# The feed-forward input GEMMs of a hybrid decoder layer, with the activations as the stationary operand

## The reference, cut to what matters

```
def swiglu(h, w_in, w_out):
    a, b = jnp.split(h @ w_in, 2, axis=-1)      # h: 256 x 2048, w_in: 2048 x 11008
    return (jax.nn.silu(a) * b) @ w_out         # w_out: 5504 x 2048

h = modulate(x, norm_ffn1[l], sh1, sc1)
x = x + 0.5 * g1 * swiglu(h, w_ffn1_in[l], w_ffn1_out[l])
...                                             # the mixer
h = modulate(x, norm_ffn2[l], sh3, sc3)
x = x + 0.5 * g3 * swiglu(h, w_ffn2_in[l], w_ffn2_out[l])
```

## Time and profile before

| what | value |
|---|---|
| median of three runs | 2865.64 us (2865.18 to 2868.14) |
| the profiled execution, first to last instruction | 2863.1 us |
| TensorE busy | 2574.2 us, 90% |
| VectorE busy | 1781.1 us, 62% |
| ScalarE busy | 997.2 us, 35% |
| transfers | 567.49 MB, mean 198 GB/s |
| mean granted TensorE clock | 0.938 of full |

### The profile page before, as it was taken

One profiled execution on the slowest core, in us unless ns is written; L12 is line 12 of the kernel. 1 busy time (PEld: TensorE's weight loads), 2 busy tenths in 40 slices (PEclk: granted clock), 3 DMA queues, 4 the chain that ended last, 5 costly groups with the idle time before them and its releaser, 6 DMA issues. The chain is left out here.

```text
span 2863.1 us, 47785 instructions
## 1 busy us (share of the span) xinstructions
PE 2574.2 (90%) x20140; PEld 2536.1 (89%) x20140; DVE 1781.1 (62%) x1754; ACT 997.2 (35%) x690; POOL 221.1 (8%) x214
## 2 busy tenths in 40 slices
PE   5589989999989788788999988989799999999897
PEld 5589989999989688688899988989699989999897
DVE  5666656767656656888777775656575545444444
ACT  1044433333333322323334443333344333333333
POOL 0010000460000112232400000000000000000000
PEclk6589999999999879889999999999899999999999
DMA  8777767777767552233346655756487645555451
GB/s 297 265 221 264 264 205 240 261 251 263 247 203 246 187 176 89 89 118 103 118 150 213 226 191 190 236 191 246 136 276 252 228 148 194 180 182 185 144 183 70
DMA packets 386137, 567.49 MB, mean 198 GB/s; under 512 B 12709, under 2 KB 209829, under 8 KB 385253
## 3 DMA queue, kind: packets, MB, share of 16 engines
q1 hardware_dynamic: 385332, 560.33, 58.1%
q0 software_dynamic: 688, 5.51, 0.6%
HBM read 561.59 MB, written 4.19 MB: 198 GB/s over the span
## 5 line engine op out<-in xcount | busy, mean ns | idle before, releaser
L264 PE MATMUL gps<-hs,whi 128*128 128x256 f32 x9088 | 1687.8, 288 | 161.9 <-DVE wlo L774 103.8
L264 PEld LDWEIGHTS gps<-hs,whi 128*128 128x128 f32 x9088 | 1446.9, 196 | 174.6 <-DVE wlo L774 107.2
L774 DVE TENSOR_TENSOR wlo<-raw,whi 128x2048 fp32r<-128x2048 f32 x400 | 925.3, 2314 | 858.9 <-ACT whi L520 858.8
L264 PE MATMUL gps<-hs,wlo 128*128 128x256 f32 x4544 | 1301.5, 286 | 0.0
L520 ACT ACTIVATE whi<-raw 128x2048 fp32r<-128x2048 f32 x400 | 765.3, 1914 | 1318.2 <-PE gps L264 1314.9
L264 PEld LDWEIGHTS gps<-hs,wlo 128*128 128x128 f32 x4544 | 888.6, 196 | 0.0
L264 PE MATMUL gps<-ffs,whi 128*128 128x256 f32 x2752 | 506.6, 287 | 27.8 <-DVE ffs L840 23.9
L264 PEld LDWEIGHTS gps<-ffs,whi 128*128 128x128 f32 x2752 | 434.6, 194 | 33.3 <-issue 24.4
L791 DVE SCALAR_TENSOR_TENSOR acc<-raw,cact,acc 128x512 f32<-128x512 f32 x508 | 384.7, 757 | 15.6
L264 PE MATMUL gps<-ffs,wlo 128*128 128x256 f32 x1376 | 392.2, 285 | 0.0
L264 PEld LDWEIGHTS gps<-ffs,wlo 128*128 128x128 f32 x1376 | 267.3, 194 | 0.0
(11 more groups left out here) (216 smaller groups left out, 1328.8 us busy)
## 6 DMA issues: line engine op xcount, KB each, us to landing
raw<-in_w_ffn_in_dram SPq DMA_DIRECT2D x336, 512.0 KB
raw<-in_w_ada_dram SPq DMA_DIRECT2D x144, 1024.0 KB
raw<-in_w_in_dram SPq DMA_DIRECT2D x80, 1024.0 KB
raw<-in_w_ffn_out_dram SPq DMA_DIRECT2D x56, 1024.0 KB
raw<-in_w_ffn_out_dram SPq DMA_DIRECT2D x40, 768.0 KB
raw<-in_w_a_proj_dram SPq DMA_DIRECT2D x16, 1024.0 KB
raw<-in_w_b_glu_dram SPq DMA_DIRECT2D x32, 512.0 KB
raw<-in_w_out_dram SPq DMA_DIRECT2D x16, 1024.0 KB
```

What stands on the lines that cost most here:

```text
L264: return pe.matmul(out, lhsT, rhs, start=start, stop=stop, skip_group_check=True)
L774: dve.tensor_tensor(wlo[:, mpos % SPLIT, :, :], raw[:, pos % RING, :, :], whi[:, mpos % SPLIT, :, :].bitcast(F32), ALU.subtract).then_inc( ...
```

## The change

In the pair phases the roles on TensorE are exchanged: `slab_pair` holds a 128 x 128 block of activations (128 features by 128 tokens, two token halves c) and moves 512 weight columns, so a slab is 2 x 4 x 3 = 24 matmuls of 512 columns. The result has tokens on the partitions. A body is now 512 gate columns in g = 0 and the matching 512 of the other half in g = 1; each slab is one transfer of 1 MB. ACT evacuates g = 0 alone (Silu to `half`, 1024 elements a partition), DVE multiplies g = 1 with it (`gated`, 1024), and the four blocks of 128 columns are turned back by eight 128 x 128 transposes on TensorE into `mps` (`turn`), then copied and split into `ffs` by ACT and DVE, 1024 elements each. A body's `turn` is issued on TensorE inside the next body (or the next output phase): after the first token half of its slab 0, or after the first column block of an output phase. It waits for `gated`. The output phase no longer waits for all of `ffs` at its start: each of its slabs waits for the bodies that made its rows. The narrow body moves 384 columns in all eight slabs. First bodies after a norm or an output phase, and first bodies of output phases, are taken out of the loops.

```diff
@@ class/plan: start is counted in tiles of ffs; Run has pt @@
@@ sync @@
+                            if ph.evac == "pair":
+                                width = COLS - P if ph.narrow else COLS
+                                parts = [(dst[:, :, 0:width],
+                                          w[:, k0:k0 + kc, bass.ds(ph.col + i * COLS + g * ph.pair, width)])]
...
@@ scalar, evacuate @@
-                    act.wait_ge(sem("prod_free"), r.p + i * 2 + g + 1)
-                    act.activation(sil[:, :, :], out[:, 0:2, :], ACT.Silu).then_inc(sem("silu_ready"), 1)
-                    act.wait_ge(psum_free(b), q)
...
+                    if g == 0:
+                        act.wait_ge(sem("prod_free"), r.p + i + 1)
+                        act.activation(half[:, :, 0:width], out.rearrange("p (c h) s -> p c (h s)", c=2)[:, :, 0:width],
+                                       ACT.Silu).then_inc(psum_free(b), 1)
+                    else:
+                        act.wait_ge(sem("ff_turned"), r.pt + i + 1)
+                        turned = mps[:, 0:2, :].rearrange("p a (b s) -> p (a b) s", b=2)
+                        act.activation(ffs[:, bass.ds(ph.start + 4 * i, blocks), 0, :], turned[:, 0:blocks, :], ACT.Copy
+                                       ).then_inc(sem("ff_hi"), 1)
@@ vector, evacuate @@
+                    if g == 1:
+                        dve.wait_ge(slab_done, m_end)
+                        dve.wait_ge(psum_free(0), q)
+                        dve.tensor_tensor(gated[:, :, 0:width], half[:, :, 0:width],
+                                          out.rearrange("p (c h) s -> p c (h s)", c=2)[:, :, 0:width], ALU.mult
+                                          ).then_inc(psum_free(b), 1)
+                        dve.wait_ge(sem("ff_hi"), r.p + i + 1)
+                        turned = mps[:, 0:2, :].rearrange("p a (b s) -> p (a b) s", b=2)
+                        at_ = bass.ds(ph.start + 4 * i, blocks)
+                        dve.tensor_tensor(ffs[:, at_, 1, :], turned[:, 0:blocks, :],
+                                          ffs[:, at_, 0, :].bitcast(F32), ALU.subtract).then_inc(sem("prod_free"), 1)
@@ tensor @@
-                if ph.moving == "ff":
-                    pe.wait_ge(sem("prod_free"), r.p + 1)
+                def slab_pair(g, s, mp, k0):
+                    width = COLS - P if ph.narrow else COLS
+                    for c in range(2):
+                        tok = slice(P * c, P * c + P)
+                        out = gps[:, g, 2 * c:2 * c + 2, :].rearrange("p h s -> p (h s)")[:, 0:width]
+                        for k in range(ph.chunks[s]):
+                            hi, lo = whi[:, mp % SPLIT, k, 0:width], wlo[:, mp % SPLIT, k, 0:width]
+                            xh, xl = moving[:, k0 + k, 0, tok], moving[:, k0 + k, 1, tok]
+                            mm(pe, out, xh, hi, k0 + k == 0, False)
+                            mm(pe, out, xh, lo, False, False)
+                            ins = mm(pe, out, xl, hi, False, k0 + k == NT - 1)
+                        yield ins
...
+                def turn(p, q, blocks):
+                    pe.wait_ge(psum_free(1), q)
+                    pe.wait_ge(sem("prod_free"), p + 1)
+                    for b in range(blocks):
+                        for c in range(2):
+                            at_ = S * (b % 2) + P * c
+                            ins = pe.transpose(mps[:, b // 2, at_:at_ + P], gated[:, c, P * b:P * b + P], ident[:, :])
+                    ins.then_inc(sem("ff_turned"), 1)
...
+                            if ph.moving == "ff" and head and g == 0:
+                                pe.wait_ge(sem("prod_free"), ff_from[0] + (k0 + ph.chunks[s] + 3) // 4 + 1)
+                            parts = slab_pair(g, s, mp, k0) if ph.evac == "pair" else slab_plain(g, s, mp, k0)
+                            for j, ins in enumerate(parts):
+                                if s == 0 and j == 0 and g == 0 and (not head or owed[0]):
+                                    if ph.evac == "pair":
+                                        turn(r.p + i - 1, r.q + i, owed[0] if head else 4)
+                                    elif head:
+                                        turn(r.p - 1, r.q, owed[0])
```

More of the change, by code:

```diff
@@ L85, in ffn @@
             Phase("in", win, 0, NT, 4, "pair", "h", True, pair=FF),
-            Phase("in", win, 4 * COLS, NT, FF1 // 4 - 4, "pair", "h", False, pair=FF, start=8)]
+            Phase("in", win, 4 * COLS, NT, FF1 // 4 - 4, "pair", "h", False, pair=FF, start=16)]
         steps = [("gemm", p) for p in first]
@@ L92, in ffn @@
             Phase("in", win, FF1 * P, NT, (FT - FF1) // 4, "pair", "h", ada, pair=FF),
-            Phase("in", win, (FT - 3) * P, NT, 1, "pair", "h", ada, pair=FF, start=(FT - 3 - FF1) // 2, narrow=True),
+            Phase("in", win, (FT - 3) * P, NT, 1, "pair", "h", ada, pair=FF, start=FT - 3 - FF1, narrow=True),
             Phase("out", wout, 0, FT - FF1, 2, "resid", "ff", ada, gate=gate, row=FF1 * P, last=(n == 2)))]
@@ L117, in __init__ @@
     def __init__(self):
-        self.n = self.m = self.q = self.c = self.p = self.g = 0
+        self.n = self.m = self.q = self.c = self.p = self.pt = 0
 def build(nc, a):
@@ L199, in build @@
         prod = at("prod", T + 2 * K, [P, 2, S])
+        half = at("half", W + 12 * K, [P, 2, COLS])
+        gated = at("gated", T, [P, 2, COLS])
         acc = at("acc", T + 4 * K, [P, COLS])
@@ L324, in body @@
                             dst = raw[:, pos % RING, 0:kc, :]
-                            if ph.pair:
-                                width = P if (ph.narrow and g == 1) else COLS // 2
+                            if ph.evac == "pair":
+                                width = COLS - P if ph.narrow else COLS
+                                parts = [(dst[:, :, 0:width],
+                                          w[:, k0:k0 + kc, bass.ds(ph.col + i * COLS + g * ph.pair, width)])]
+                            elif ph.pair:
+                                width = COLS // 2
                                 col = ph.col + (i * 2 + g) * (COLS // 2)
@@ L507, in _ @@
             pool.wait_ge(sem("x_saved"), 16)
-            pool.wait_ge(sem("prod_free"), 1 + FT // 2 + 1 + D // (COLS // 2))
+            pool.wait_ge(sem("prod_free"), 1 + (FT + 3) // 4 + D // (COLS // 2))
             pool.dma_start(xT[:, :, :].rearrange("p t s -> p (t s)"), x_kept).then_inc(sem("x_back"), 16)
@@ L560, in evacuate @@
                 if ph.evac == "pair":
-                    act.wait_ge(sem("prod_free"), r.p + i * 2 + g + 1)
-                    act.activation(sil[:, :, :], out[:, 0:2, :], ACT.Silu).then_inc(sem("silu_ready"), 1)
-                    act.wait_ge(psum_free(b), q)
[L564 to L568, removed]
+                    width = COLS - P if ph.narrow else COLS
+                    blocks = width // P
+                    if g == 0:
[7 more added lines that the diff above has]
+                                       ).then_inc(sem("ff_hi"), 1)
                 elif ph.evac == "conv":
@@ L625, in gemm @@
                 r.q += ph.bodies
-                if ph.evac in ("pair", "glu"):
-                    r.p += 2 * ph.bodies
+                r.p += {"pair": ph.bodies, "glu": 2 * ph.bodies}.get(ph.evac, 0)
+                r.pt += ph.bodies * (ph.evac == "pair")
             def norm(k, last=False):
@@ L875, in evacuate @@
                     t = bass.ds(4 * i + 2 * g, 2)
-                    dve.wait_ge(sem("silu_ready"), p + 1)
+                    dve.wait_ge(sem("silu_ready"), i * 2 + g + 1)
                     dve.tensor_tensor(prod[:, :, :], sil[:, :, :], out[:, 0:2, :], ALU.mult).then_inc(psum_free(b), 1)
@@ L1192, in _ @@
             r = Run()
+            owed, ff_from = [0], [0]
             def ada_end(c, used, fresh=True):
@@ L1231, in gemm @@
                 moving = {"h": hs, "ff": ffs, "yb": ybs}[ph.moving]
-                if ph.moving == "ff":
-                    pe.wait_ge(sem("prod_free"), r.p + 1)
-                elif ph.name == "w_out":
+                if ph.evac == "pair" and not owed[0]:
+                    ff_from[0] = r.p
+                if ph.name == "w_out":
                     pe.wait_ge(sem("prod_free"), r.p + 1)
@@ L1240, in gemm, with slab_plain @@
                     pe.wait_ge(sem("y_lo"), 2)
+                def slab_pair(g, s, mp, k0):
+                    width = COLS - P if ph.narrow else COLS
+                    for c in range(2):
[8 more added lines that the diff above has]
+                        yield ins
+                def slab_plain(g, s, mp, k0):
+                    for j in range(4):
+                        for k in range(ph.chunks[s]):
+                            hi = whi[:, mp % SPLIT, k, P * j:P * j + P]
+                            lo = wlo[:, mp % SPLIT, k, P * j:P * j + P]
+                            xh, xl = moving[:, k0 + k, 0, :], moving[:, k0 + k, 1, :]
```

(20 more changed lines are left out.)

## The result

The changed kernel takes 2845.09 us (2842.94 to 2848.83, four runs) against 2865.41 beside it: ratio 0.9927, interval 0.9913 to 0.9941. It is 20.3 us faster where 55 were forecast. The sign, the new wait and its length came out as worked; the price of a matmul and the count of half-clock stretches did not.

What follows compares the result with a forecast made beforehand. TensorE was taken to set the pace in the feed-forward phases, busy for 90% of the span. The terms summed to 75.5 us, less 20.4 for the clock: 55.1 us saved, 2810 us forecast, range 2788 to 2856.

Steps and rivals of the forecast that it cites:

- (a): Slabs of full bodies: 24 matmuls at 0.216 us replace 48 at 0.120, saving 91.6 us.
- (b): Ada bodies: TensorE's pause before slab 6 goes, 1.5 us in each of 14 and 1.2 in one more; 22.2 us saved.
- (c): The new transposes: eight at 0.109 us of TensorE per body, 18 full bodies; 15.7 us lost.
- (d): `turn` waits for `gated`, queued on DVE behind slab 1's subtraction: 3.1 us non-ada, 2.1 ada; 37.6 us lost.
- (e): Start of output phases after full bodies: waits of 5.9 or 6.6 us become 3.3 or 4.2; 5.1 us saved.
- (f): Two narrow bodies, slab 7 of the body before to output phase: from 51.4 and 46.6 us; 9.9 us saved.
- (h): Half clock after the new pauses: 12 falls among 18 pauses, 1.7 us lost each, 20.4 us in all.
- The price of a matmul: A 512-column fp32r matmul on TensorE steps at 216 ns, taken from plain float32; bounds 213.3 and 240.
- Rival 2: The 11 ns above a bare step belong to the fp32r matmul: 227 ns, gain 14 us, 2851 us; chance 0.11.
- rival 3: fp32r columns cost 120 ns per 256, so 240 per matmul: 35.0 us slower, 2901 us; chance 0.08.
- Rival 4: Transfers or DVE hold ada bodies at today's 48.56 us: gain 17 us, 2848 us; chance 0.06.
- non-ada bodies gain nothing: Sign of being right: non-ada bodies take 45 to 47 us, so they gain next to nothing.

Runs made afterwards that it cites:

- half_load: The changed kernel with 64 instead of 128 tokens as stationary operand of each input matmul, half of the tokens left out; 2845.21 us, one run.
- banks: The changed kernel with a slab's two token halves interleaved matmul by matmul, so neighbouring matmuls add to different PSUM banks; 2847.7 us, one run.
- turn_twice: The changed kernel with each block of transposes issued twice, the second writing the same values; 2864.52 us over ten runs.
- gate_early: The changed kernel with `gated` computed between the subtractions of the next body's slabs 0 and 1 instead of behind both; 2775.27 us.
- turn_late: The changed kernel with the transposes issued after the whole of slab 0 instead of after its first half; 2790.31 us.

## Why the prediction was wrong, by its own steps

| step | predicted us | measured us | from |
|---|---|---|---|
| (a) columns | +91.6 | +50.5 | 3840 x 13.3 ns, less cold starts |
| (b) pause before slab 6 | +22.2 | +21.9 | gone in 14 bodies; 2.51 became 1.58 |
| (c) transposes | -15.7 | -15.7 | steps of 109 ns |
| (d) waits for `gated` | -37.6 | -36.5 | 16 records of 1.86 (one 2.23) and 2.82, 0.16 added to each |
| (e) output phases | +5.1 | +5.2 | 5.86 and 6.64 became 3.19 and 4.09 |
| (f) narrow bodies | +9.9 | +3.9 | 51.4 and 46.6 became 48.1 and 46.0 |
| (h) clock | -20.4 | -6.8 | three falls, one of double length: 4 x 1.7; the narrow bodies' two are within (f) |
| sum | 55.1 | 22.5 | the span shrank by 23.0 |

**The step that failed is "The price of a matmul".** It took the plain float32 step of 216 ns "as the row with the same occupation". The measured step is 227 ns: an fp32r matmul carries 13.3 ns beyond its columns at either width, which the 120 of the earlier trace rows already held. With it term (a) is 50.5 us instead of 91.6, 41.1 short, more than the 32.6 by which the whole sum was off; the other terms together erred the other way. Plain float32 at the same occupation carries 2.7. The explanation offered in the prediction, weight load and columns of equal length getting in each other's way, fell with half_load: the extra is there when the load has half the columns and the matmul twice those of before. Rival 2 had this mechanism, with 11 ns (120 less the 109 of a plain step) in place of the 13.3 that 120 less 106.7 gives. It was given 0.11, though every fp32r row fitted it (and rival 3 as well), and the row against it was of another type.

**The clock (h) was overpriced.** 5 of the 18 pauses were followed by the half clock in the profiled execution (one of the 12 after ada bodies, two of four non-ada ones, both into narrow bodies), not 12. The rows had said it: the prediction itself put the recorded pause after ada bodies at 2.0 us, on the border of two classes, and took 7 of 12 where the class below 2 us had 2 of 9. With 2 of 9 it would have been three. The mistake ran the other way from (a) and hid 13.6 us of it, which is luck. Which of the pauses has a fall is not fixed by their length: in the traces of half_load, banks and turn_twice, which have the same 18 pauses to within 0.2 us, 1, 7 and 4 of them were followed by the half clock, and 8 of these 12 were not among the five here. What else decides it is open. The spread goes with it, 5.9 us over four runs of the changed kernel and 11.5 over ten of turn_twice against 2.6 for gate_early, which has no such fall.

**Narrow bodies (f).** Slabs of 24 x 0.173 = 4.2 us instead of 3.9, and a half-clock stretch after each of the two pauses into them, which the forecast had put under (h). How the 6.0 us that (f) lacks divide between the two is not shown.

**What held.** (b) and (c) to 0.3 us; (d) to 1 us, from rows of a kernel without that wait. Rival 4 is out: no wait of TensorE is put down to transfers in an ada body, at 266 GB/s. ACT does wait for weights twice in one such body (5.6 and 3.5 us, at 551.99 and 557.42), and TensorE has no pause behind it. Rival 3 is out by the step of 227. That non-ada bodies gain nothing also held, and more: 2586.70 less 2539.24 gives a body of 47.5 us without the half clock, 2539.24 less 2490.95 one of 48.3 with part of it, where a body of before took 46.2; the forecast had 45 to 47.

## What to carry to other kernels

Price an instruction of a new width from rows of its own type at another width, as a line with a fixed part, and take the fixed part from the column time; a row of another type with the same occupation is only a bound. When a step is added between engines, look where it stands in the queue of the engine that makes it: here one multiplication queued behind a subtraction that it does not need cost more than the transposes, and moving it by one place turned a gain of 20 us into one of 90. And read which class of observed pauses a forecast one falls in before counting falls of the clock.

## What the runs showed of the hardware

- An fp32r matmul steps at 120, 173 and 227 ns for 256, 384 and 512 moving columns at the full clock: columns at 2.4 GHz plus 13.3 ns. At the half clock the step of 512 columns was 427 ns, the columns alone. With 64 instead of 128 stationary columns it was 230 at the full clock, with neighbouring matmuls in different banks 227.
- Of the 12 pauses of TensorE of 1.9 to 2.2 us after ada bodies, 1, 1, 4 and 2 were followed by the half clock in the traces of the changed kernel, half_load, banks and turn_twice; of the 10 others, 2.0 to 4.1 us, 8, 2, 6 and 6. The five of 1.3 to 1.4 us in turn_late had none, nor had the 13 of that length before slab 6 in the kernel before. A stretch of half clock in the changed kernel's feed-forward phases was 3.4 us, once 6.8.
- 172 further transposes in steps of 109 ns brought no further fall of the clock (8 against 9).
